# RMS norms by feature chunk, their scale and shift split between VectorE and ScalarE, and squares behind the experts by token tile

## The reference, cut to what matters

```python
def _rms_norm(x, g):
    y = x * rsqrt(mean(x * x, axis=-1) + EPS)
    return y * g
...
hp = _rms_norm(xp, norm1_g[i]) * (1.0 + sc1p) + sh1p
hs = _rms_norm(xs, norm1_g[i]) * (1.0 + sc1s) + sh1s
...
xp = xp + g1p * op
xs = xs + g1s * os_
hp = _rms_norm(xp, norm2_g[i]) * (1.0 + sc2p) + sh2p
hs = _rms_norm(xs, norm2_g[i]) * (1.0 + sc2s) + sh2s
xp = xp + g2p * _moe(hp, ...)
xs = xs + g2s * _moe(hs, ...)
```

## Time and profile before

| what | value |
|---|---|
| median of three runs | 1942.0 us (1938.81 to 1945.7) |
| profiled execution | 1946.48 us |
| span of its rows | 1944.7 us, 20950 instructions |
| PE busy | 1678.6 us (86% of the span) |
| DVE busy | 539.6 us (28%) |
| ACT busy | 454.4 us (23%) |
| POOL busy | 147.3 us (8%) |
| mean granted TensorE clock | 0.898 of full speed |

### The profile page before, as it was taken

The page is one execution under the profiler, slowest core; times in us unless marked ns, Lnnn a source line. Parts: engine busy times, 40 slices in busy tenths (PEclk is TensorE's granted clock), DMA queues, the critical chain, the costliest instruction groups (busy, mean ns, idle before and its releaser), DMA issues.

```text
span 1944.7 us, 20950 instructions
## 1 busy us (share of the span) xinstructions
PE 1678.6 (86%) x7808; PEld 1040.4 (54%) x7808; DVE 539.6 (28%) x1293; ACT 454.4 (23%) x835; POOL 147.3 (8%) x188
## 2 busy tenths in 40 slices
PE   5699999988998999797799999578898859999984
PEld 3354688874556888554543333436666535433323
DVE  1556233434733424203200000154233240000002
ACT  1144421222444212101111111133323121111111
POOL 0000011110100111000100000102222000000001
PEclk7799896888998979798899999878999879999996
DMA  9021224032213273015579999410200355999972
GB/s 370 33 98 65 87 109 195 23 131 75 78 69 124 90 266 145 15 41 236 191 305 401 406 405 400 153 73 11 113 33 15 131 226 216 370 404 405 398 288 104
DMA packets 65336, 354.80 MB, mean 182 GB/s; under 512 B 7952, under 2 KB 8208, under 8 KB 28240
## 3 DMA queue, kind: packets, MB, share of 16 engines
q1 hardware_dynamic: 47888, 316.70, 41.3%
q10 hardware_dynamic: 13888, 24.13, 3.7%
q0 software_dynamic: 3456, 12.58, 1.8%
HBM read 331.87 MB, written 27.27 MB: 185 GB/s over the span
## 4 chain that ended last, share of the span: by engine, by line
PE 72%; DMA 9%; DVE 8%; ACT 5%; issue 4%; SPq 1%; ACTq 0%; DVEq 0%; POOL 0%; POOLq 0%
PE bank L663 10%; PE bank L893 8%; PE bank L911 5%; DMA ring<-ws 5%; PE bank L944 4%; PE bank L827 4%; PE bank L762 4%; PE bank L746 4%; PE bank L1098 4%; DMA work<-ws 3%; PE bank L590 3%; PE bank L956 2%; PE bank L1164 2%; PE bank L611 2%; PE bank L770 2%
## 5 line engine op out<-in xcount | busy, mean ns | idle before, releaser
L663 PE MATMUL bank<-hT,ring 128*128 128x384 f32 x768 | 265.9, 505 | 17.0 <-issue 11.0
L663 PEld LDWEIGHTS bank<-hT,ring 128*128 128x128 f32 x768 | 149.6, 198 | 124.8 <-issue 24.3
L1098 PE MATMUL bank<-hT,ring 128*128 128x384 f32 x256 | 92.6, 527 | 15.1 <-ACT work L1504 13.5
L893 PE MATMUL bank<-ring,work 128*128 128x512 f32 x192 | 89.3, 618 | 12.3 <-DMA ring<-ws 12.1
L2017 DVE TENSOR_TENSOR work<-bank,work 128x512 f32<-128x512 f32 x12 | 8.3, 693 | 304.3 <-PE bank L893 304.3
L827 PE MATMUL bank<-mix,ring 128*128 128x384 f32 x256 | 84.7, 494 | 8.7 <-DVE mix L1887 8.7
L893 PE MATMUL bank<-work 128*128 128x512 f32 x192 | 85.5, 596 | 6.2 <-DMA work<-ws 6.0
L590 PE MATMUL bank<-ring,small 128*32 128x256 f32 x768 | 69.4, 496 | 19.4 <-DMA ring<-ws 19.4
L762 PEld LDWEIGHTS bank<-work 128*128 128x128 f32 x576 | 78.7, 219 | 8.9 <-issue 8.9
L762 PE MATMUL bank<-work 128*128 128x64 f32 x576 | 83.2, 306 | 0.0
L911 PE MATMUL bank<-work 128*64 128x512 f32 x320 | 76.6, 597 | 6.9 <-DMA work<-ws 6.9
(11 more groups left out here) (354 smaller groups left out, 2459.8 us busy)
## 6 DMA issues: line engine op xcount, KB each, us to landing
ring<-ws SPq DMA_DIRECT2D x192, 1024.0 KB, 9.7
work<-ws SPq DMA_DIRECT2D x96, 1024.0 KB, 14.6
y_slots<-work ACTq DMA_DIRECT2D x24, 256.0 KB, 7.1
x_slots<-s_gla SPq DMA_DIRECT2D x22, 256.0 KB, 6.7
work<-x_slots ACTq DMA_DIRECT2D x40, 128.0 KB, 6.7
y_slots<-work ACTq DMA_DIRECT2D x40, 128.0 KB, 7.6
work<-x_slots ACTq DMA_DIRECT2D x16, 256.0 KB, 7.9
work<-lruw_in ACTq DMA_DIRECT2D x8, 256.0 KB, 2.8
```

Of the source, the lines that this page charges most:

```text
L663: last = mm(bank[b % 2][:, 0:T], w[:, b % 2, k, :], hT[:, k, :], start=(k == 0), stop=(k == KD - 1))
L893: last = mm(bank[2 + kind][:], xg[p % 2][:, k, :], w[:, k % 4, :], start=(k == 0), stop=(k == KD - 1))
L1098: last = mm(bank[2 * i + m][:, 0:T], w[:, m, k, :], hT[:, k, :], start=(k == 0), stop=(k == KD - 1))
```

## The change

- `norm` on DVE makes `gain` ahead of the wait for `rstd`. The multiply by `rstd` goes chunk by chunk, eight instructions of 128x384. DVE scales and shifts chunks 0, 3 and 6, each behind the multiply of the chunk after it.
- ACT scales and shifts chunks 1, 2, 4, 5 and 7 (Identity with scale and shift read from tiles, two instructions a chunk, as soon as the chunk's multiply is done). A new semaphore `h_scalar` counts ACT's chunks, `h_ready` now counts DVE's. At its end `norm` on DVE waits for ACT's five.
- PE waits chunk by chunk (`wait_h`) in the tail matmuls, the router and the GLA's gate rows.
- For norms 2 and 4 ACT squares by token tile: three instructions of 128x8x128, each behind its tile's `acc_added`; PE sums them with 24 matmuls of 128 columns (`mean_square_tiles`), in the place where `mean_square` stood.
- Norm 4's multiply by `rstd` goes in eight instructions, all ahead of the eight that follow.
- `router_sig` is merged into `logits_read`.

```diff
+NORM_ACT = (1, 2, 4, 5, 7)
+NORM_DVE = (0, 3, 6)
+SQ_BASE = (0, 8, 16, 19, 27)
...
+            def wait_h(n, k):
+
+                if k in NORM_DVE:
+                    pe.wait_ge(h_ready, len(NORM_DVE) * n + NORM_DVE.index(k) + 1)
+                else:
+                    pe.wait_ge(h_scalar, len(NORM_ACT) * n + NORM_ACT.index(k) + 1)
+
+            def mean_square_tiles(n):
+
+                for t in range(NT):
+                    pe.wait_ge(sq_done, SQ_BASE[n] + t + 1)
+                    for k in range(KD):
+                        last = mm(bank[6][:, t * P:(t + 1) * P], ones, squares[:, k, t * P:(t + 1) * P],
+                                  start=(k == 0), stop=(k == KD - 1))
+                last.then_inc(ms_done, 1)
...
             mean_square(0)
-            pe.wait_ge(h_ready, 1)
-
             pe.wait_ge(tail_loaded, 16)
             for k in range(KD):
+                wait_h(0, k)
                 last = mm(bank[7][:, 0:T], tw[:, k, :], hT[:, k, :], start=(k == 0), stop=(k == KD - 1))
...
-                    act.wait_ge(x_ready, n)
-                for k in range(KD):
+                    for t in range(NT):
+                        act.wait_ge(acc_added, 2 * t + 2 + 6 * (n // 2 - 1))
+                        A(squares[:, :, t * P:(t + 1) * P], xT[:, :, t * P:(t + 1) * P], ACT.Square)\
+                            .then_inc(sq_done, 1)
+                for k in range(KD if n % 2 or n == 0 else 0):
...
+                if n < 4:
+                    sh = mod[n // 2][:, 24 * (n % 2):24 * (n % 2) + 8, :]
+                    for k in NORM_ACT:
+                        act.wait_ge(normed_done, 10 * n + k + 3)
+                        for q, t0, tn in SEGS:
+                            src, dst = normed[:, k, t0:t0 + tn], hT[:, k, t0:t0 + tn]
...
+                            last = A(dst, src, ACT.Identity, scale=gain[:, k, q:q + 1], bias=sh[:, k, q:q + 1])
+                        last.then_inc(h_scalar, 1)
...
-                dve.wait_ge(rstd_done, n + 1)
...
                 TT(gain, gain, bc3(gn, 2), ALU.mult).then_inc(normed_done, 1)
-                TT(normed, xT[:], bcm(rstd, KD), ALU.mult).then_inc(normed_done, 1)
-                dve.wait_ge(normed_done, 3 * n + 3)
-                for k in range(KD):
+                dve.wait_ge(rstd_done, n + 1)
+
+                def affine(k):
+
+                    dve.wait_ge(normed_done, 10 * n + k + 3)
...
+                for k in range(KD):
+                    TT(normed[:, k, :], xT[:, k, :], rstd, ALU.mult).then_inc(normed_done, 1)
+                    if k - 1 in NORM_DVE:
+                        affine(k - 1)
+                dve.wait_ge(h_scalar, len(NORM_ACT) * (n + 1))
```

More of the change, by code:

```diff
@@ L346, in build @@
         h_ready = sem("h_ready")
+        h_scalar = sem("h_scalar")
         x_ready = sem("x_ready")
@@ L412, in build @@
         router_done = sem("router_done")
-        router_sig = sem("router_sig")
         logits_read = sem("logits_read")
@@ L833, in experts @@
             def experts(layer):
-                pe.wait_ge(h_ready, 2 * layer + 2)
                 for k in range(KD):
+                    wait_h(2 * layer + 1, k)
                     j, pair = 32 * (k % 4), rw[:, k - k % 2:k - k % 2 + 2, :].rearrange("p a e -> p (a e)")
@@ L845, in experts @@
                         if t == 0 and half == 1:
-                            pe.wait_ge(logits_read, layer + 1)
+                            pe.wait_ge(logits_read, 2 * layer + 1)
                             for u in range(NT):
@@ L1074, in gla @@
             def gla():
-                pe.wait_ge(h_ready, 3)
                 pe.wait_ge(tail_loaded, 48)
                 for k in range(KD):
+                    wait_h(2, k)
                     last = mm(bank[7][:, 0:T], tw2[:, k, :], hT[:, k, :], start=(k == 0), stop=(k == KD - 1))
@@ L1170, in _ @@
             experts(0)
-            mean_square(2)
+            mean_square_tiles(2)
             gla()
@@ L1174, in _ @@
             experts(1)
-            mean_square(4)
+            mean_square_tiles(4)
         @block.scalar
@@ L1202, in norm @@
                 A(rstd, rstd, ACT.Exp, scale=-0.5).then_inc(rstd_done, 1)
+                if n < 4:
[4 more added lines that the diff above has]
+                            src, dst = normed[:, k, t0:t0 + tn], hT[:, k, t0:t0 + tn]
+                            if n == 2 and q:
+                                src = src.rearrange("p (r w) -> p w r", w=GRID_W)
+                                dst = dst.rearrange("p (w r) -> p w r", w=GRID_W)
+                            last = A(dst, src, ACT.Identity, scale=gain[:, k, q:q + 1], bias=sh[:, k, q:q + 1])
+                        last.then_inc(h_scalar, 1)
             norm(0)
@@ L1346, in experts @@
                 act.wait_ge(router_done, 4 * layer + 2)
-                A(rt_s.rearrange("p a b -> p (a b)"), bank[7][:, 0:NT * E], ACT.Sigmoid).then_inc(router_sig, 1)
+                A(rt_s.rearrange("p a b -> p (a b)"), bank[7][:, 0:NT * E], ACT.Sigmoid).then_inc(logits_read, 1)
                 act.wait_ge(router_done, 4 * layer + 3)
@@ L1646, in norm @@
                         last = TS(dst, src, gain[:, k, q:q + 1], sh[:, k, q:q + 1], ALU.mult, ALU.add)
-                last.then_inc(h_ready, 1)
+                    last.then_inc(h_ready, 1)
+                for k in range(KD):
[3 more added lines that the diff above has]
+                dve.wait_ge(h_scalar, len(NORM_ACT) * (n + 1))
             dve.sem_inc(mod_read, 1)
@@ L1904, in route @@
                 flat = lambda a: a.rearrange("p a b -> p (a b)")
-                dve.wait_ge(router_sig, layer + 1)
+                dve.wait_ge(logits_read, 2 * layer + 2)
                 L(TT(rt_sel, rt_s, bcm(v("rb"), NT), ALU.add))
@@ L1982, in experts @@
             def experts(layer):
-                dve.wait_ge(h_ready, 2 * layer + 2)
+                dve.wait_ge(h_ready, len(NORM_DVE) * (2 * layer + 2))
                 TS(ex_ids, cc("i16"), 1024.0, None, ALU.add)
@@ L2170, in _ @@
             dve.wait_ge(rstd_done, 5)
-            TT(normed, xT[:], bcm(rstd, KD), ALU.mult).then_inc(normed_done, 1)
-            dve.wait_ge(normed_done, 13)
             for k in range(KD):
+                TT(normed[:, k, :], xT[:, k, :], rstd, ALU.mult).then_inc(normed_done, 1)
+            for k in range(KD):
+                dve.wait_ge(normed_done, 40 + k + 1)
                 last = TS(hT[:, k, :], normed[:, k, :], v("nf", k, k + 1), None, ALU.mult)
```

6 lines of the change are left out of this document (4 added, 2 removed).

## The result

Four runs of the changed kernel gave 1928.48, 1907.61, 1926.35 and 1926.87 us, median 1926.61, beside a median of 1943.85 for the kernel before: 0.9886 of it, 95% interval 0.986 to 0.9911. That is 17.2 us less, where 20.7 were forecast. The forecast time of 1921 us is 5.6 too low; the measured median lies inside the range of 1911 to 1930. Runs over 1.5% above the fastest of the same kernel, two of e2's and one of a2's further down, are left out of medians and ratios. The profiled execution took 1928.48 us with a span of 1926.7, 18.0 less than the span before.

A forecast was written before the change was run, and what follows sets the result against it. PE bounds the kernel with 72% of the chain, standing still about 11 us in each norm. 6.8 + 7.4 + 7.4 - 0.4 - 0.5 = 20.7 us off 1942.0 gives 1921 us, range 1911 to 1930.

The forecast's parts named there:

- Norms 0 and 2: Tail and gate rows: PE starts at the first chunk after R (DVE gets `rstd`), 6.8 and 7.4 us earlier.
- ACT's share: Scale and shift in norms 0 to 3: ACT takes 0.87 us a chunk, between 0.60 and 1.29, and waits for DVE.
- rival 3: Norms 0 to 3: ACT's chunk takes twice as long, 1.74 us, giving 1930 us in all; chance 6%.
- Norms 1 and 3: Routers: the last chunk sets the end, 7.55 us after R instead of 11.26; 3.7 us each, 7.4 together.
- The rule of the Trainium skill against ACT: Multiplies and adds belong on VectorE; with all chunks on DVE the router norms would give 1.2 us each, not 3.7.
- Squares by tile: Norms 2 and 4: nothing gained, since PE's sum starts about 4.1 us after the last addition, set by its branch skip.
- The tile sums: Norms 2 and 4: 48 passes of 128 columns instead of 16 of 384 cost 0.2 us more each, 0.4 in all.
- Norm 4: Eight multiplies ahead of the first output chunk take 3.9 us for 3.36: 0.5 us lost, between 0.1 and 1.2.
- Rival 2: Norms 0 and 2: PE stays at 2.4 GHz or gets there sooner, 3.4 and 3.0 us more, 1914.6; chance 10%.

The follow-up runs named there:

- e2: Changed kernel, but PE waits for all eight chunks before its first matmul behind norms 0 to 3; median 1932.39 us, ratio 0.9932 to the kernel before.
- a2: The changed kernel run again with no edit, a third time; median 1924.99 us, ratio 0.9882 to the kernel before.
- e1: The kernel before with only the tile squares and tile sums in norms 2 and 4; median 1943.3 us, ratio 1.0001 to the kernel before.
- e3: Changed kernel, but DVE scales and shifts all eight chunks of norms 0 to 3, ACT none; median 1921.88 us, ratio 0.99 to the kernel before.
- e8: The same kernel as e3, run again beside a2; median 1926.46 us, ratio 0.9898 to the kernel before.
- e9: e7 with DVE alone scaling and shifting all chunks of norms 0 to 3; median 1903.04 us, ratio 0.9788 to the kernel before.
- a1: The changed kernel run again with no edit, a second time; median 1927.44 us, ratio 0.9906 to the kernel before.
- e7: e6 plus six unread matmuls behind the sums of squares of norms 0, 1 and 3; median 1902.27 us, ratio 0.98 to the kernel before.
- e4: Changed kernel with the sums of norms 2 and 4 inside the experts' branch, ahead of PE's wait for the last addition; median 1913.33 us, ratio 0.9832.
- e6: e4 with norm 4 shared: DVE scales the even chunks, ACT the odd ones; median 1910.91 us, ratio 0.9835 to the kernel before.
- e5: Changed kernel plus six unread matmuls of 384 columns behind the sums of squares of norms 0 to 3; median 1917.39 us, ratio 0.9873.

## Why the prediction was right, and where its steps were off

**Norms 0 and 2**, the two largest terms: 6.80 and 7.47 us against 6.8 and 7.4. The mechanism holds: PE starts at R + 1.75 and 1.84 (forecast 1.65 and 1.75), its clock starts low, and the work behind follows. In norm 0 the clock rises where it rose before. In norm 2 it rises sooner, so the gate rows take 7.09 us and not the 7.93 that were forecast, but the next eight matmuls then take 7.41 for 6.73, and the two nearly cancel. That 6.80 is so near to 6.8 also has to do with which executions were profiled: the tail took 8.46 and 8.38 us in these two, but 7.00 in e1, whose norm 0 is that of the kernel before, and 6.93 in a2. Like with like the gain is the same, 19.3 - 12.5 = 6.8. e2 confirms the early start: without it the two norms lose 4.1 and 5.1.

**ACT's share.** A chunk took 4.95 / 5 = 0.99 us on ACT with its waits for DVE, near the 0.87 taken from L1238; rival 3 (1.74) is out. Eight of DVE's multiplies in a row took 3.83, that is 0.48 each, where 0.47 was taken.

**Norms 1 and 3**: 3.7 each was too little; 5.08 and 4.43 were measured up to the experts' first matmul. In norm 1 the router ends near the forecast (7.37 for 7.55). What the step left out is that PE comes out of the longer router at 2.4 GHz, so the first eight transposes behind it took 1.09 us for 1.97. In norm 3 the clock rose inside the router, which ended at 6.90, 0.65 before the forecast; the transposes took 1.09 for 1.39.

**The rule of the Trainium skill against ACT** ("ScalarE: Activation LUTs", "Rules for kernel authors"): the prediction set 1.2 us by it against 3.7. In the stages the prediction is right, since e3, e8 and e9 lose 2.0 to 2.5 in each router. In the whole time, three pairs (a1 and e3, a2 and e8, e7 and e9) show no gain from ACT's share that can be told. One part of the reason is seen: in the five profiles in which the router takes the shared chunks one by one and PE has no extra matmuls ahead of it, experts 0 take 315.7 to 316.5 us, in the eight others 313.4 to 314.6. So norm 1's 2.0 us come back there. The granted clock of the first 14 us is 0.75 in the five and 0.81 to 0.86 in the eight (columns as above, the changed kernel first, then e3):

```profile
926.70:940.70 14.00, 12.98 (x91) 12.98 (x92) 3.40 (x16) 1.80 (x3) 4.39 (x5) 0.75 0.56 219
```

```profile
922.60:936.60 14.00, 13.04 (x97) 12.82 (x98) 3.41 (x16) 2.02 (x4) 4.33 (x5) 0.83 0.55 217
```

Why the clock is lower there is open. What becomes of norm 3's share is not seen: experts 1 take 315.1 and 316.4 us in a1 and a2, 315.4 and 316.1 in e3 and e8.

**Squares by tile**: nothing gained, as forecast, and for the reason given (e1, e4). 18 places in these profiles show 4.03 to 4.72 us from the last addition to the sum, where 4.1 was forecast, and 3.3 to 4.0 of that is the compare-and-branch. The prediction set this against the 51 and 108 ns of the Trainium skill, "Advanced Engine Details and Errata", "Control Flow Timing"; here the rows decide. **The tile sums were mis-sized**: 0.2 us each was taken, since the slow stretch was assumed to end after as much time as before. It did in 6 of 16 places (6.97 to 7.25 us a sum, before 7.02 and 7.20); in the other 10 the low clock held longer and the sum took 8.24 to 9.60.

**Norm 4**: 0.36 lost, forecast 0.5.

**The sum** is closer than its terms. Norms 0 to 3 gained 23.8 us from R on, 2.2 more than forecast; the sums of squares and norm 4 lost 1.0 more than forecast; and 3.9 were lost where nothing was forecast. In part these cancel.

**What no step had**: the +3.9 us of the stretches whose code did not change. The mixer took 829.7 to 836.8 us and the GLA 271.7 to 286.7 over thirteen profiles, a1 and a2 showing 282.0 and 271.7 for one kernel. The single run of 1907.61 us had a granted clock of 0.914, the other three 0.901 and 0.902, which fits; it was not the one profiled. The prediction allowed about 5 us either way for scatter, and the result lay 5.6 from its 1921. That the mixer came out at 836.7 in the first two profiles of the changed kernel and 835.2 in the third, all above the 833.4 before, is not shown to be the change's doing: e4 and e6 have the same code up to there and took 835.5 and 831.8. What sets the clock there stays open.

**Rival 2** did not come true: in every profile without extra matmuls PE started the tail low, behind 4.24 us of pause in the first, though in a2, e4 and e6 the clock rose sooner in it (6.84 to 7.09 us). Behind 0.37 us of pause (e5, e7, e9) it stays at 2.4 GHz, and the price of it in norm 0, 3.4 us in the prediction, was 2.8 in e5 and 1.3 between e6 and e7.

## What to carry to other kernels

Where a bound engine waits for a whole tensor, let it start at the first chunk: at its slow clock it needs longer a chunk than the makers do, and the wait nearly vanishes; helping the makers with another engine is then worth much less. When a wait keeps the same distance to something else than the releaser that the profile names, believe the distance, and move the work to the other side of that something: the sums ahead of the branch's end gave 14 us where squaring earlier gave nothing. Count a saving stage by stage, and expect the clock in unchanged loops to move the total by as much as a small term.

## What the runs showed of the hardware

- From the last addition across a branch not taken, PE's next matmul came 4.03 to 4.72 us later in 18 places. The compare-and-branch took 3.3 to 4.0 of that and ended 1.3 to 1.5 us after a 16 KB packet on an instruction queue.
- The same GLA code took 271.7 or 282.0 us in two executions of one kernel; the granted clock of one 30 us stretch was 0.94 or 0.72.
- Behind six unread matmuls (4.03 us) in the pause ahead of it, the tail ran at 2.4 GHz from its first pass and took 5.58 us; without them it took 6.84 to 8.45 in five profiles with the same tail.
